# A feed-forward output stage on one Trainium2 core: first weight splits moved between evictions, the last tiles of a group in another order, one eviction moved ahead

## The reference

```
a_ff, g_ff = jnp.split(xn2 @ p['w_up'], 2, axis=-1)         # 1024 -> 2 * 2816
g_ff = dwconv2d_grid(g_ff, ...) (latent) / dwconv1d(...) (context)
x = x + gate2 * ((jax.nn.gelu(g_ff) * a_ff) @ p['w_down'])  # 2816 -> 1024
y = rms_norm(x, g_final)
```

## Time and profile before

| what | value |
|---|---|
| runs | 3065.35 us (3064.91 to 3068.18) |
| profiled execution, its own time | 3065.72 us |
| span inside it | 3063.9 us |
| TensorE matmul busy | 2879.0 us, 94% |
| VectorE, ScalarE, GpSimd busy | 1566.6, 962.3, 675.3 us |
| down stage, from the end of the factor products to the end | about 2511 to 3063.9 us |

### The profile page before, as it was taken

The page is one execution under the profiler, slowest core; times in us unless marked ns, Lnnn a source line. Parts: engine busy times, 40 slices in busy tenths (PEclk is TensorE's granted clock), DMA queues, the critical chain, the costliest instruction groups (busy, mean ns, idle before and its releaser), DMA issues.

```text
span 3063.9 us, 38426 instructions
## 1 busy us (share of the span) xinstructions
PE 2879.0 (94%) x15332; PEld 2411.3 (79%) x15332; DVE 1566.6 (51%) x1730; ACT 962.3 (31%) x1630; POOL 675.3 (22%) x348
## 2 busy tenths in 40 slices
PE   5999999979999985999899999999999999999998
PEld 2878787867778765777788888888888888777786
DVE  6764664535555543555654645646546464223214
ACT  5443533236666663555301001010010013111112
POOL 3132333202222223444222222222222220000000
PEclk7999999989999997999999999999999999999999
DMA  6211211477766664254211111111111125322222
GB/s 234 70 60 65 81 69 62 127 250 217 222 199 198 199 196 130 96 163 142 92 57 50 35 56 50 35 50 48 44 50 35 56 88 178 110 81 73 68 83 77
DMA packets 184717, 321.36 MB, mean 105 GB/s; under 512 B 21454, under 2 KB 128334, under 8 KB 175310
## 3 DMA queue, kind: packets, MB, share of 16 engines
q1 hardware_dynamic: 161840, 270.35, 27.4%
q10 hardware_dynamic: 22752, 49.29, 4.9%
HBM read 210.07 MB, written 109.52 MB: 104 GB/s over the span
## 4 chain that ended last, share of the span: by engine, by line
PE 50%; DVE 5%; ACT 2%; DMA 2%; issue 1%; POOL 0%; SPq 0%; DVEq 0%; ACTq 0%; POOLq 0%
PE out_up_banks L2252 32%; PE out_up_banks L1701 16%; PE out_up_banks L2242 2%; DVE ffn_hidden L2409 1%; DVE residual L2346 1%; DVE ffn_hidden L2343 1%; PE out_up_banks L2223 1%; ACT ffn_hidden L2082 1%; DMA up_w_whole<-w_up_in 0%; ACT ffn_hidden L2089 0%; DMA out_w_whole<-w_out_in 0%; DVE down_gated L1806 0%; DVE ffn_hidden L2337 0%; DMA normed<-normed_dram 0%; DMA down_h<-hidden_ff_dram 0%
## 5 line engine op out<-in xcount | busy, mean ns | idle before, releaser
L2252 PE MATMUL out_up_banks<-xh_rest,up_w_hi 128*128 128x512 f32 (+2 forms) x1408 | 493.6, 351 | 10.5 <-DVE xl_rest L2363 8.4
L2252 PE MATMUL out_up_banks<-xh_rest,up_w_lo 128*128 128x512 f32 (+2 forms) x1408 | 493.8, 351 | 0.0
L2252 PE MATMUL out_up_banks<-xl_rest,up_w_hi 128*128 128x512 f32 (+2 forms) x1408 | 493.6, 351 | 0.0
L2409 DVE SCALAR_TENSOR_TENSOR ffn_hidden<-grid,params,ffn_hidden 128x2048 f32<-128x2048 f32 x176 | 462.0, 2625 | 24.6 <-DVE ffn_hidden L2406 0.2
L1701 PE MATMUL out_up_banks<-down_w,down_h_hi 128*128 128x512 f32 x952 | 299.7, 396 | 2.3 <-DVE down_h_lo L1778 2.3
L2252 PEld LDWEIGHTS out_up_banks<-xh_rest,up_w_hi 128*128 128x128 f32 x1408 | 266.4, 189 | 41.8 <-DVE xl_rest L2363 9.2
L136 POOL TENSOR_TENSOR up_w_hi<-up_w_whole,zero 128x1024 fp32r<-128x1024 f32 x44 | 124.1, 2820 | 781.1 <-PE out_up_banks L2252 762.9
L2252 PEld LDWEIGHTS out_up_banks<-xl_rest,up_w_hi 128*128 128x128 f32 x1408 | 266.1, 189 | 30.4
L2252 PEld LDWEIGHTS out_up_banks<-xh_rest,up_w_lo 128*128 128x128 f32 x1408 | 266.2, 189 | 28.0
L1778 DVE TENSOR_TENSOR down_h_lo<-down_h,down_h_hi 128x384 fp32r<-128x384 f32 (+1 forms) x152 | 72.9, 481 | 343.1 <-ACT down_h_hi L1743 343.1
L2406 DVE TENSOR_SCALAR ffn_hidden<-grid,params 128x2048 f32<-128x2048 f32 x22 | 49.5, 2250 | 372.2 <-ACT line L2126 372.2
(11 more groups left out here) (276 smaller groups left out, 5553.2 us busy)
## 6 DMA issues: line engine op xcount, KB each, us to landing
hidden_ff_dram<-ffn_hidden SPq DMA_DIRECT2D x22, 1088.0 KB, 4.9
up_w_whole<-w_up_in SPq DMA_DIRECT2D x44, 512.0 KB, 5.2
down_h<-hidden_ff_dram SPq DMA_DIRECT2D x88, 192.0 KB, 2.4
swap_f_first_dram<-f_sent ACTq DMA_DIRECT2D x64, 256.0 KB, 5.1
f_spectrum<-swap_f_first_dram SPq DMA_DIRECT2D x64, 256.0 KB, 5.1
swap_first_dram<-hy_sent ACTq DMA_DIRECT2D x64, 256.0 KB, 3.8
hy_spectrum<-swap_first_dram SPq DMA_DIRECT2D x64, 256.0 KB, 5.6
pre_dram<-in_result SPq DMA_DIRECT2D x15, 1088.0 KB, 4.0
```

Source lines behind the costliest of these rows:

```text
L2252: last = pe.matmul(out, weight[:, u, k], in_block(value, rest, b, k), start=(k == 0 and j == 0), stop=(k == KM - 1 and j == 2))
L2409: last = nc.vector.scalar_tensor_tensor(out=y, in0=window, scalar=weight, in1=y, op0=ALU.mult, op1=ALU.add)
```

## The change

Four edits, all in the last tile of the up stage and in the down stage:

1. **Early splits between evictions.** `scalar_early` takes one piece at a time, and is called after gate evictions b = 0 and b = 1 of f = 21, not after all of them.
2. **Early loads inside the loop.** SyncE's first three weight and hidden loads (nine transfers) are issued after the third turn of its loop (EARLY_HIDDEN = 3), when the first three hidden tiles have been stored; the loop is cut in two.
3. **Order of tiles at a group's end.** The last six tiles of a group of three are (20,0) (21,0) (20,1) (20,2) (21,1) (21,2), before they were (20,0) (20,1) (20,2) (21,0) (21,1) (21,2).
4. **First eviction ahead.** The eviction of a group's first tile is done in step k = 21 of its own group, the second and third at k = 0 and 1 of the next (in the first group of one tile at k = 0 and 3).

```diff
+EARLY_HIDDEN = 3
 def down_work(g):
+    first = {KF - 1: DOWN_GROUPS[g][0]} if len(DOWN_GROUPS[g]) == 3 else {}
     if g == 0:
-        return {kind: {} for kind in kinds}
+        return {kind: first if kind == "evict" else {} for kind in kinds}
     if len(DOWN_GROUPS[g]) == 3:
-        at = ((0, 1, 2), (3, 4, 5), ...
+        at = ((0, 1), (3, 4, 5), ...
     elif len(before) == 3:
-        at = ((0, 3, 6), (8, 12, 16), ...
+        at = ((0, 3), (8, 12, 16), ...
+    work["evict"] = dict(zip(at[0], before[-len(at[0]):])) | first
...
+    def sync_early(sp):
+        sp.wait_ge(up["lo_ready"], TT)
+        for u in range(3):
+            sp.wait_ge(up["x_stored"][u], 16 * len(range(u, TT, 3)))
+        sp.wait_ge(up["h_stored"], 16 * (EARLY_HIDDEN + 1))
+        for k in range(3):
+            load_w(sp, k)
+            load_h(sp, k)
...
-        for n in range(2):
-            ready(n)
-            tile(n, 0)
-        for n in range(2):
-            for at in range(1, 3):
-                tile(n, at)
-        for n in range(2, len(steps)):
-            ready(n)
-            for at in range(len(DOWN_GROUPS[steps[n][0]])):
-                tile(n, at)
+        for g, group in enumerate(DOWN_GROUPS):
+            order = [(k, at) for k in range(KF) for at in range(len(group))]
+            if g == 0:
+                order[:6] = [(0, 0), (1, 0), (0, 1), (0, 2), (1, 1), (1, 2)]
+            if len(group) == 3:
+                order[-6:] = [(KF - 2, 0), (KF - 1, 0), (KF - 2, 1), (KF - 2, 2), (KF - 1, 1), (KF - 1, 2)]
+            for k, at in order:
+                if at == 0:
+                    ready(g * KF + k)
+                tile(g * KF + k, at)

-    def scalar_early(act):
-        for k in range(2):
-            split_w(act, k)
-            h_high(act, k)
+    def scalar_early(act, k):
+        split_w(act, k)
+        h_high(act, k)
...
             low_part(nc.vector, dve, k)
+        evict(0)
         for n in range(KF, len(steps)):
...
-                with sp.Fori(1, KF) as f:
+                with sp.Fori(1, EARLY_HIDDEN + 1) as f:
+                    tile(f)
+                down["sync_early"](sp)
+                with sp.Fori(EARLY_HIDDEN + 1, KF) as f:
+                    tile(f)
...
-                    if early:
-                        early(act)
+                        if early and b < W_EARLY:
+                            early(act, b)
```

More of the change, by code:

```diff
@@ L1550, in down_work @@
     kinds = ("evict", "square", "mean", "root", "scale", "store", "load")
+    first = {KF - 1: DOWN_GROUPS[g][0]} if len(DOWN_GROUPS[g]) == 3 else {}
     if g == 0:
-        return {kind: {} for kind in kinds}
+        return {kind: first if kind == "evict" else {} for kind in kinds}
     before = DOWN_GROUPS[g - 1]
     if len(DOWN_GROUPS[g]) == 3:
-        at = ((0, 1, 2), (3, 4, 5), (3, 4, 5), (3, 4, 5), (3, 4, 5), (6, 8, 10), (11, 13, 15))
+        at = ((0, 1), (3, 4, 5), (3, 4, 5), (3, 4, 5), (3, 4, 5), (6, 8, 10), (11, 13, 15))
     elif len(before) == 3:
-        at = ((0, 3, 6), (8, 12, 16), (9, 13, 17), (10, 14, 18), (11, 15, 19), (14, 18, 21), (19,))
+        at = ((0, 3), (8, 12, 16), (9, 13, 17), (10, 14, 18), (11, 15, 19), (14, 18, 21), (19,))
     else:
@@ L1618, in spare, with load_h, load_w @@
         return banks.rearrange("p (s n) c -> p s (n c)", n=2)[:, pair]
-    def sync(sp):
-        def load_h(n):
-            g, k = steps[n]
-            if n >= 3:
-                sp.wait_ge(h_ready, n - 2)
-            for to, at, w in tokens(g):
-                sp.dma_start(h[:, n % 3, to:to + w], d["hidden_ff"][k][:, at:at + w]).then_inc(h_loaded[n % 3], 16)
-        def load_w(k):
-            if k >= 3:
-                sp.wait_ge(w_ready, k - 2)
-            sp.dma_start(x(k % 3), d["w_down"][k]).then_inc(w_loaded[k % 3], 16)
+    def load_h(sp, n):
+        g, k = steps[n]
+        if n >= 3:
+            sp.wait_ge(h_ready, n - 2)
+        for to, at, w in tokens(g):
+            sp.dma_start(h[:, n % 3, to:to + w], d["hidden_ff"][k][:, at:at + w]).then_inc(h_loaded[n % 3], 16)
+    def load_w(sp, k):
+        if k >= 3:
+            sp.wait_ge(w_ready, k - 2)
+        sp.dma_start(x(k % 3), d["w_down"][k]).then_inc(w_loaded[k % 3], 16)
+    def sync_early(sp):
[6 more added lines that the diff above has]
+            load_h(sp, k)
+    def sync(sp):
         def load_x(i):
@@ L1643, in store @@
             sp.dma_start(d["y"][DOWN_ORDER[i]], x(i % 4)).then_inc(stored[i % 4], 16)
-        sp.wait_ge(up["lo_ready"], TT)
-        for u in range(3):
-            sp.wait_ge(up["x_stored"][u], 16 * len(range(u, TT, 3)))
-        for k in range(3):
-            load_w(k)
-            load_h(k)
         for k in range(3, 5):
-            load_w(k)
-            load_h(k)
+            load_w(sp, k)
+            load_h(sp, k)
         sp.wait_ge(up["h_ready"], KF)
@@ L1669, in sync @@
             g, k = steps[n]
-            load_h(n)
+            load_h(sp, n)
             if (g, k) == (1, 1):
@@ L1850, in vector @@
                                            in1=gain[:, cols], op0=ALU.mult, op1=ALU.mult).then_inc(result_ready, 1)
-    return {"sync": sync, "tensor": tensor, "scalar_early": scalar_early, "scalar": scalar,
+    return {"sync_early": sync_early, "sync": sync, "tensor": tensor, "scalar_early": scalar_early, "scalar": scalar,
             "gpsimd_early": gpsimd_early, "vector": vector}
@@ L2038, in _, with tile @@
                     load_xn(t)
-                with sp.Fori(1, KF) as f:
+                def tile(f):
                     for u in range(2):
```

## The result

The changed kernel takes 3047.63 us (median of four runs, 3046.42 to 3048.35), beside it the kernel before takes 3066.76 us (3064.91 to 3069.36): a ratio of 0.9937 [0.9919, 0.9954]. The forecast was 3051.2 us with a range from 3048.3 us. Two repeats further down both give 0.9952 ([0.9938, 0.9965] and [0.9939, 0.9964]), 14.7 us of 3064 us.

The account below looks back on a forecast made before the run. TensorE is busy 94% of the span, so only its pauses and clock can give time. 6.06 + 6.46 + 2.07 + 0.53 - 0.60 = 14.5 us off 3065.72 us gives 3051.2 us, range 3048.3 to 3057.5.

Parts of the forecast that it names:

- taps quick, first pause and its low clock gone: Start of the down stage: with GpSimd idle VectorE's taps run quicker, so TensorE's wait and low clock go, 6.06 us gained.
- end of group 0: Where group 0 turns into group 1: loss falls from 8.61 to 2.15 us, 6.46 us gained if the clock stays up.
- second tile at groups 1 to 3: Ends of groups 1 to 3: the wait for the second tile's bank goes, 3 x 0.69 = 2.07 us gained.
- new order, five ends: Five group ends: step 21's pieces come 0.12 us later than one tile of step 20, 0.60 us lost.
- end of group 4, first single tile to step 16: End of group 4: three evictions behind the group's end become two, 0.53 us gained.
- The first place: Pause between last factor products and down stage: GpSimd's early pieces slow VectorE's taps; moving them gains 6.06 us.
- the delay of 2.15 us at the end of group 0: Start of group 1: tile 2 is due at G + 2.8 but may start at G + 4.9, with 2.0 us idle.
- the rival that rested on the missing row: End of group 0: clock falls after a 2 us pause, costing 2.8 us; chance 0.14, shared with more wait at ends.
- the bounds of the terms: Limits on single terms, such as first place 0 to 6.06 us gained, new order 0 to 6.1 us lost.
- Short pauses that bring the clock down at every group end: Five group ends: the 0.1 us waits each cost 2.8 us, 14 us in all, 3065.3 us, no change; chance 0.03.
- The slower rival: Five group ends: 1.23 us wait for step 21's pieces plus low clock, 5.2 us slower, 3070.9 us; chance 0.03.
- The early loads: Up stage: nine transfers go out about 850 us earlier, delaying up weights within 18 us of cover; cost 0.

Follow-up runs that it names:

- early_only: Kernel before with only the early splits between evictions and the early loads inside the loop: 3056.72 us, 0.9974 of the kernel before.
- ends_only: Kernel before with only the new order of tiles at group ends and the first eviction ahead: 3055.62 us, 0.9971 of the kernel before.
- pool_busy: Changed kernel plus six GpSimd instructions, results unused, beside VectorE's taps of the last tile: 3051.92 us, 0.9964 of the kernel before.
- after_again: The changed kernel, unchanged, profiled a second time: 3049.28 us, 0.9952 of the kernel before.
- after_third: The changed kernel, unchanged, run once more: 3050.82 us, 0.9952 of the kernel before.
- better: Changed kernel with (21,0) behind two tiles of step 20 at ends of groups 1 to 4, and single-tile evictions by halves: 3044.57 us, 0.9942 of before.
- evict_only: Kernel before with only the first eviction ahead, order of tiles as before: 3059.21 us, 0.9984 of the kernel before.
- loads_only: Kernel before with only SyncE's loop cut in two and the nine early loads between its halves: 3063.87 us, 1.0000 of the kernel before.

## Why the prediction was right, and where it failed

By its own terms, lost time in the trace of before against that of after:

| term | forecast | measured |
|---|---|---|
| taps quick, first pause and its low clock gone | 6.06 | 6.06 (nothing left) |
| end of group 0 | 6.46 | 8.62 - 0.55 = 8.1 |
| second tile at groups 1 to 3 | 2.07 | 2.4 |
| new order, five ends | -0.60 | 5 x 0.20 = -1.0 |
| end of group 4, first single tile to step 16 | 0.53 | 0.6 |
| single tiles from step 17 | none | -1.0 |
| sum | 14.5 | 15.1 |
| ahead of the down stage | none | 3.5 |

**Two steps failed.** The one that put the time outside the range is the range itself: it gave nothing to the time ahead of the down stage, where 3.5 us moved, and nothing to the scatter of executions. In the sum the mis-sized term is the delay at the end of group 0. That the sum, 14.5 us, is still within 0.6 us of the 15.1 us measured is in part luck: 1.6 us more at the end of group 0 and 0.3 us at groups 1 to 3 stand against 1.4 us less from the new order and the last single tiles.

**The first place** is right in its cause, by early_only, ends_only and pool_busy. That its size agrees to the hundredth says little, as the forecast took the whole loss from the same trace; in five other traces with slow taps the place loses from 5.8 to 7.2 us.

**The failed term is the delay of 2.15 us at the end of group 0**, and in it the wait: tile 0's eviction was to wait for the x tile until G - 4.1, with G the group's end. It measured 0.55 us: 0.45 us of delay and 0.10 us behind it. I took 5.5 us, the median that the view gives for three transfers issued together, for the first of them. That one lands sooner: below 4.4 us in the changed kernel, and 4.53 us in pool_busy, where VectorE waited for it at 2600.02 behind the issue at 2595.49:

```profile
2600.02 0.69 DVE L1820 TENSOR_TENSOR down_gated<-out_up_banks,down_gate 128x512 f32<-128x512 f32 x1 [1.98 <-DMA down_x<-x_dram]
```

Bound by TensorE's tile, the eviction starts 5.4 us before the group's end (2594.92 against 2600.32) and not 4.1, 1.3 us earlier, and the gate row takes 4.2 and not 4.6 us, 0.4 us less: 1.7 us, against the 1.6 us that the delay was off. The 1.3 us repeat: in after_again, after_third, ends_only and better the eviction also waits for TensorE's tile, 4.4 us behind the issue of its x tile. The 0.4 us don't: the gate row takes 4.0 to 4.7 us in these traces, and 0.35 to 1.03 us are lost there, in each of them less than half of the forecast delay. The clock didn't fall; with 0.29 us of idle time the changed kernel did not put that to the test, but evict_only did, at 1.93 us, and the rival that rested on the missing row falls.

**The new order** costs 0.12 us at each end as worked out, and 0.08 us more on the tile behind it: a waiting TensorE loses about 0.1 us beyond the wait itself. The same shows at groups 1 to 3, where 0.69 us were in truth 0.79. The single tiles from step 17 on lost 2.42 us where the trace of before has 1.46 us. This is the landing of one hidden load, 4.57 us in the chain; it is scatter and of no edit's making, since after_again and after_third, the same kernel, have 1.40 and 1.39 us there.

**The range**, the first of the two failed steps, was built from the bounds of the terms alone. These held: 15.1 us is within what they allow, and both repeats, 3049.28 and 3050.82 us, are inside it. What it left out is the scatter of the executions ahead of the down stage. The forecast started from one median of three runs, 3065.35 us, and from a profile 0.37 us above it, while larger sets have 3064.16, 3064.38 and 3063.83 us, and a set of four runs can be 3 us off. The standard deviation in these sets is 2.6 to 3.0 us, so the median of three or four runs, before as after, is easily 1.5 to 2 us off (an estimate from these deviations), and the low end should have been about 3046 us. One trace can't show this scatter, but the three runs of before already spread over 3.3 us.

**The rivals.** Short pauses that bring the clock down at every group end: in the changed kernel there are five of 0.12 us, one of 0.3 us and four of 0.5 to 1.1 us, and over the whole stage the granted clock is 1.00. By the rule of the Trainium skill, page "TensorE: Matmul & The Clock Gate", section "A second HAM failure mode: psum-queue depth-cycling", the clock of such a kernel would swing. The trace here does not agree: 1.00 through the stage. The slower rival, a wait of 1.23 us and a low clock at each of five ends, is off by a factor of ten in the wait (0.12 us). Edit 3 taken by itself does turn out slower, 1.0011, though by a wait that I had not named. The early loads cost nothing: no wait of TensorE over 1 us in the up products after 1533 us in any of the traces, until the down stage begins, and 1.0000 for loads_only.

## What to carry to other kernels

Two engines that look independent in the code can slow each other: where a chain of one is slow for a stretch, look at what starts and ends with that stretch on the others, and move that work to where the chain is idle. A reordering and the work moved into the room that it makes can be worth much together and nothing, or less, apart, so a test of parts has to take such a pair as one. A range for a change of 0.5% has to hold the scatter of executions beside the bounds of the terms, and a transfer's landing is read for the one that is waited for, not from the median of its batch.

## What the runs showed of the hardware

- VectorE beside GpSimd: taps of 128x2048 from 2.45 to 3.9 us each, the one-input first tap from 1.35 to 2.15 us (pool_busy), a 128x128 row from 0.34 to 1.03 and 1.31 us; GpSimd's four splits from 6.8 to 13.3 us.
- After 1.93 us of idle time TensorE's granted clock was 1.00; behind 4.2 and 5.1 us it was 0.51 and 0.50, behind 4.24 us 0.50 in ends_only, and behind 4.31 us 0.61 over a stretch in pool_busy.
- Of 512 KB transfers at the end of group 0, the first of the x tiles issued together was there within 4.4 to 4.5 us, where the view's median for the batch is 5.5 us; the gate row, issued alone, took 3.9 to 4.7 us in the traces here.
- The same code, unchanged, put the start of the down stage anywhere from 2503.1 to 2512.8 us (the three executions of the changed kernel). What makes it, beyond the one place shown, stays open.
